# A two-block network on one core: first-stage transfers and matmul parts in a new order, key tiles in homes of their own

## The reference

```
mod = silu(c) @ w_ada + b_ada                    # c: 1 x 1024, w_ada: 1024 x 6144
shift1, scale1, gate1, shift2, scale2, gate2 = split(mod, 6)
h = x * (1 + scale1) + shift1                    # x: 256 x 1024
q, k, v, z, xbc, dt_raw, g = split(h @ w_in)     # q, k, v: 1024 columns each
...                                              # attention, scan, gating, experts, two more layers
```

## Time and profile before

| | |
|---|---|
| time, median of 3 runs | 1861.02 us (1858.63 to 1865.48) |
| the profiled execution's own time | 1863.23 us |
| its span | 1861.4 us |
| TensorE matmul busy | 1684.5 us (90%) |
| VectorE busy | 915.7 us (49%) |
| ScalarE busy | 568.4 us (31%) |
| mean granted TensorE clock | 0.965 of full |
| DMA | 563.19 MB, mean 303 GB/s |

### The profile page before, as it was taken

One profiled execution on the slowest core, in us unless ns is written; L12 is line 12 of the kernel. 1 busy time (PEld: TensorE's weight loads), 2 busy tenths in 40 slices (PEclk: granted clock), 3 DMA queues, 4 the chain that ended last, 5 costly groups with the idle time before them and its releaser, 6 DMA issues.

```text
span 1861.4 us, 30972 instructions
## 1 busy us (share of the span) xinstructions
PE 1684.5 (90%) x12554; PEld 1596.1 (86%) x12554; DVE 915.7 (49%) x2285; ACT 568.4 (31%) x1528; POOL 326.9 (18%) x301
## 2 busy tenths in 40 slices
PE   4999999999989888888898899777799999999998
PEld 4789878888888888877898899776699999989998
DVE  5642375651447666666877754469634210331200
ACT  0111223840135444434564321235513100132000
POOL 0100000000024444344423312126300000020000
PEclk9998999999999999989999999888899999999999
DMA  8963348354189999999999999999876888745783
GB/s 363 374 234 112 114 125 257 118 224 144 46 328 377 420 417 418 421 420 420 416 420 411 420 420 408 421 382 382 328 266 250 325 294 295 251 176 207 272 293 133
DMA packets 85437, 563.19 MB, mean 303 GB/s; under 512 B 8832, under 2 KB 17568, under 8 KB 17968
## 3 DMA queue, kind: packets, MB, share of 16 engines
q0 software_dynamic: 39776, 289.46, 38.0%
q1 hardware_dynamic: 38416, 251.85, 36.4%
q10 hardware_dynamic: 7104, 19.92, 3.4%
HBM read 556.96 MB, written 4.23 MB: 301 GB/s over the span
## 4 chain that ended last, share of the span: by engine, by line
PE 68%; DMA 15%; DVE 7%; ACT 6%; issue 3%; POOL 0%; SPq 0%; ACTq 0%; DVEq 0%; POOLq 0%
PE PS L965 30%; PE PS L655 19%; PE PS L944 8%; DMA AUX<-in_peer_uv_dram,SCR 4%; DMA V<-in_peer_uv_dram,SCR 4%; DMA CONV<-in_peer_uv_dram,SCR 4%; DMA ring<-in_stream_dram 3%; PE PS L726 1%; DVE PROJ L2203 1%; PE PS L701 1%; PE PS L677 1%; PE PS L859 1%; ACT L1503 1%; ACT PROJ L1518 1%; DVE SCR L2140 1%
## 5 line engine op out<-in xcount | busy, mean ns | idle before, releaser
L944 PE MATMUL PS<-PROJ,AUX 128*128 128x128 f32 x1712 | 223.5, 290 | 67.5 <-ACT PROJ L1518 67.3
L655 PE MATMUL PS<-H,ring 128*128 128x256 f32 x1216 | 274.9, 387 | 4.4 <-DMA ring<-in_stream_dram 4.4
L944 PEld LDWEIGHTS PS<-PROJ,AUX 128*128 128x128 f32 x1712 | 211.9, 203 | 75.4 <-ACT PROJ L1518 74.9
L655 PEld LDWEIGHTS PS<-H,ring 128*128 128x128 f32 x1216 | 235.2, 195 | 38.4 <-issue 5.9
L965 PE MATMUL PS<-H,ring 128*128 128x128 f32 x2272 | 261.7, 276 | 3.9 <-DMA ring<-in_stream_dram 2.2
L965 PEld LDWEIGHTS PS<-H,ring 128*128 128x128 f32 x2272 | 258.2, 193 | 5.1 <-issue 4.2
L1301 POOL DMA_INDIRECT AUX<-in_peer_uv_dram,SCR x124 | 138.9, 1120 | 485.1 <-PE PS L944 254.2
L944 PE MATMUL PS<-PROJ,CONV 128*128 128x128 f32 x1248 | 166.9, 294 | 41.7 <-ACT PROJ L1518 41.6
L944 PEld LDWEIGHTS PS<-PROJ,CONV 128*128 128x128 f32 x1248 | 159.7, 209 | 45.7 <-ACT PROJ L1518 45.5
L965 PE MATMUL PS<-PROJ,ring 128*128 128x128 f32 x1664 | 191.4, 275 | 2.7 <-DMA ring<-in_stream_dram 2.7
L965 PEld LDWEIGHTS PS<-PROJ,ring 128*128 128x128 f32 x1664 | 188.6, 192 | 3.8 <-DMA ring<-in_stream_dram 3.4
(11 more groups left out here) (351 smaller groups left out, 2033.5 us busy)
## 6 DMA issues: line engine op xcount, KB each, us to landing
ring<-in_stream_dram SPq DMA_DIRECT2D x181, 1024.0 KB
AUX<-in_stream_dram SPq DMA_DIRECT2D x51, 1024.0 KB, 4.8
AUX<-in_ada_dram POOLq DMA_DIRECT2D x16, 1024.0 KB, 9.4
PROJ<-in_ada_dram ACTq DMA_DIRECT2D x4, 1024.0 KB, 20.3
AUX<-in_ada_dram SPq DMA_DIRECT2D x4, 1024.0 KB, 20.0
AUX<-in_stream_dram ACTq DMA_DIRECT2D x4, 1024.0 KB, 8.3
bias_skewed<-AUX ACTq DMA_DIRECT2D x1, 3072.0 KB, 43.5
ring<-in_stream_dram ACTq DMA_DIRECT2D x2, 1024.0 KB
```

What stands on the lines that cost most here:

```text
L655: mm = pe.matmul(acc(n, c), w[:, k, c * P:(c + 1) * P], src[:, g * DC + k, :], start=(g == 0 and k == 0 and (c == 0 or groups == 1)), stop ...
L944: mm = pe.matmul(y_chunk(t, c), UV[b][:, D + c * P:D + (c + 1) * P], DIAG[turn % ND], start=(k == 0 and c % 4 == 0), stop=(k == SPT - 1), ...
```

## The change

Four edits, all in the first stage.

1. The four key tiles no longer pass through `ring`. They are loaded by ScalarE, behind its other first issues, into `KEY_HOMES`: three regions of `PROJ` (chunks 40 to 63) and all of `V`, which hold nothing yet at that time. TensorE waits for all four before the first key tile. The ring's counts are lowered by one to fit; SP's loop over the stream starts with the value tiles, and its waits on `tile_used` are as before.
2. The order of the first issues: SP gets `par`, shift 0, `X`, query 0, shift 1, query 2, shift 2, shift 3; ScalarE gets scale 0, `con`, scale 1, query 1, scale 2, query 3, scale 3, `rows`, `wdt` and the four key tiles. `con` is now counted with `X` and not with `par`; ScalarE's `silu(c)` waits for `par` alone but stands behind 13 issues; TensorE, GpSimd and `modulated(0)` wait for `X` and `con`.
3. On VectorE the first half of pair 2 moves ahead of `modulated(1)`.
4. The parts of the query projection are in another order around the column sums.

```diff
 def place(e):
-    before = FRONT // SLOTS if slot < SLOTS else 0
+    before = FRONT // SLOTS - 1 if slot < SLOTS else 0
...
+        KEY_HOMES = [flat(PROJ[:, 40:48, :]), flat(PROJ[:, 48:56, :]), flat(PROJ[:, 56:64, :]), flat(V[:, :, :])]
...
             shift_tile(0)
             sp.dma_start(X[:, :, :], io["xT"]).then_inc(S("x_landed"), 16)
+            query_tile(0)
             shift_tile(1)
-            query_tile(0)
+            query_tile(2)
             shift_tile(2)
-            query_tile(2)
             shift_tile(3)
-            with sp.Fori(1, TILE0["query"] // SLOTS) as i:
+            with sp.Fori(2, TILE0["query"] // SLOTS) as i:
...
             def tile_wait(name, i):
                 t = TILE0[name] + i
-                pe.wait_ge(S(f"tile_landed{t % SLOTS}"), 16 * (t // SLOTS + 1))
+                if name == "k":
+                    pe.wait_ge(S("homes_landed"), 64)
+                    return KEY_HOMES[i].rearrange("p (k n) -> p k n", k=DC)
+                pe.wait_ge(S(f"tile_landed{t % SLOTS}"), 16 * (t // SLOTS + (1 if name == "q" else 0)))
...
-            pe.wait_ge(S("params_landed"), 32)
+            pe.wait_ge(S("x_landed"), 32)
...
             early_sums(0)
             query_part((0, 1), (0, 1))
             early_sums(1)
+            query_part((2,), (0, 1))
             query_part((0, 1), (2, 3))
-            query_part((2,), (0, 1, 2, 3))
             early_sums(2)
-            query_part((0, 1), (4, 5))
+            query_part((2,), (2, 3))
+            query_part((3,), (0, 1))
             early_sums(3)
-            query_part((3,), (0, 1, 2, 3))
-            query_part((2, 3), (4, 5))
+            query_part((3,), (2, 3))
+            query_part((0, 1, 2, 3), (4, 5))
             query_part((0, 1, 2, 3), (6, 7))
...
-            act.dma_start(con[:, :], io["con"]).then_inc(S("params_landed"), 16)
             scale_tile(0)
-            act.dma_start(rows[:, :], io["rows"]).then_inc(S("rows_landed"), 16)
+            act.dma_start(con[:, :], io["con"]).then_inc(S("x_landed"), 16)
             scale_tile(1)
             query_tile(1)
             scale_tile(2)
+            query_tile(3)
             scale_tile(3)
-            query_tile(3)
+            act.dma_start(rows[:, :], io["rows"]).then_inc(S("rows_landed"), 16)
             act.dma_start(wdt[:, :, :], io["wdt"]).then_inc(S("wdt_landed"), 16)
-            act.wait_ge(S("params_landed"), 32)
+            for t in range(4):
+                act.dma_start(KEY_HOMES[t], io["stream"][TILE0["k"] + t]).then_inc(S("homes_landed"), 16)
+            act.wait_ge(S("params_landed"), 16)
...
             def ada_pair(p, ks=range(DC)):
...
             ada_pair(1)
+            ada_pair(2, range(0, 4))
             modulated(1)
-            ada_pair(2)
+            ada_pair(2, range(4, DC))
```

More of the change, by code:

```diff
@@ L852, in out_tile @@
                 if u == 0 and t == 0:
-                    pe.wait_ge(S("out_landed"), 64)
+                    pe.wait_ge(S("homes_landed"), 128)
                 ready = taken_from("ssd") if u == 0 and t == 0 else None
@@ L1252, in _ @@
                     pool.dma_start(flat(adaW[:, s]), io["ada"][4 * i + s]).then_inc(S(f"ada_late{s}"), 16)
-            pool.wait_ge(S("params_landed"), 32)
+            pool.wait_ge(S("x_landed"), 32)
             for h in range(HEADS):
@@ L1449, in _ @@
             for t in range(4):
-                act.dma_start(out_weights(t), io["stream"][TILE0["query"] + t]).then_inc(S("out_landed"), 16)
+                act.dma_start(out_weights(t), io["stream"][TILE0["query"] + t]).then_inc(S("homes_landed"), 16)
             for c in range(16):
@@ L1833, in ada, with ada_pair @@
                             ada_step(adaW[:, s], k, CONV[:, base + s, :], k and ada_done(i, s) - 2 * (DC - k))
-            def ada_pair(p):
+            def ada_pair(p, ks=range(DC)):
                 dve.wait_ge(S(f"ada_landed{p}"), 16)
                 dve.wait_ge(S(f"ada_early{p}"), 16)
-                for k in range(DC):
+                for k in ks:
                     for j, w in enumerate((adaW[:, p], adaE[:, p])):
@@ L1857, in modulated @@
                 if p == 0:
-                    dve.wait_ge(S("x_landed"), 16)
+                    dve.wait_ge(S("x_landed"), 32)
                 for c in (2 * p, 2 * p + 1):
```

## The result

The changed kernel took 1867.8 us (median of 7 runs, 1863.36 to 1874.08) against 1863.43 us for the kernel before, measured beside it (7 runs, 1858.63 to 1865.48). The ratio is 1.0033, 95% interval 1.0017 to 1.0048: 3 to 9 us slower, where 3 us faster was forecast. The median of the kernel before is, by these 7 runs, 2.4 us above the one that the prediction stood on.

What follows compares the result with a forecast made beforehand. Bound: the first-stage path through transfers, VectorE's sums and TensorE up to the keys' end. 3.8 us late against 7.4 saved gave -3.6, taken as -3: 1858 us from the median of 1861.02, range 1851.5 to 1864.

Steps and rivals of the forecast that it cites:

- The step that failed: ScalarE's start: four added issues of about 0.5 us each, silu done near 9.4 us in place of 7.34.
- The mechanism: Rival, chance 0.07: ScalarE's tenth to thirteenth issues wait for landings, silu ends at 24.4 us, keys +3.2 us, about 1864.
- The second term: TensorE's clock behind the thin stretch, 25 to 47 us: a loss between 0 and 3.0 us.
- the 16 matmuls ahead of `early_sums(3)` warm the clock first: Argument against the clock staying low on the 36 query matmuls behind the last sums, which would take 2 to 3 us.
- The missing gap: Ahead of the key projection: no 4.4 us wait for key tiles and no slow clock behind it, 7.4 us saved.
- the order of issues and of parts: Reordering in the first stage: last sums 2.0 us late, 36 matmuls behind them, query projection ends 3.8 us later.
- shift tile 2 was read off at 32.9 us: Transfer step in SP's queue: shift tile 2 lands at 32.9 us in place of 27.8, about 5 us later.
- for this move the prediction had under half a microsecond: Moving `rows` to the end of ScalarE's queue gives that queue 0.16 MiB, under half a microsecond.
- The rival in which this delay isn't felt: Rival, chance 0.08: shift tile 2 stays near 27.8 us, total change -6 to -7.6 us, about 1854.3.
- the slow rival: Rival, chance 0.07: waiting issues in ScalarE's queue hold silu and make the kernel 3.2 us slower, about 1864.
- the clock had a chance of its own: Rival, chance 0.14: the clock stays low behind the last sums, 2 to 3 us of the gain go, about 1860.5.

Runs made afterwards that it cites:

- x2: Kernel before with only the key tiles loaded to their homes, their issues ahead of silu; 1863.32 us, ratio 0.9994.
- x4: Kernel before, keys through the ring, plus four loads of 128 partitions by 8 bytes issued by ScalarE ahead of silu; 1868.72 us, one run.
- x5: Kernel before, keys through the ring, plus four loads of 16 partitions by 8 bytes issued by ScalarE ahead of silu; 1861.24 us, one run.
- r3_after: The changed kernel executed once more, nothing altered; 1871.98 us.
- x1: Changed kernel with silu moved ahead of ScalarE's four key-tile issues, nothing else; 1865.61 us, ratio 1.0001.
- x6: Changed kernel with the four key tiles issued by SP behind shift 3 in place of ScalarE; 1866.13 us, ratio 1.0014.
- x8: x3 with the changed kernel's order of first issues on SP and ScalarE, and `con` counted with `X`; 1863.04 us, ratio 0.9994.
- x3: Kernel before with only the key tiles loaded to their homes, silu ahead of their issues; 1858.43 us, ratio 0.9972.
- x7: x3 with VectorE's first half of pair 2 ahead of `modulated(1)` and the query parts in another order; 1859.53 us, ratio 0.9979.

## Why the prediction was wrong

**The step that failed.** "ScalarE issues 13 transfers in place of 9 before `silu`. The ninth cost 0.47 us; four more of about 0.5 put the end of `silu` from 7.34 to about 9.4 us." The four cost 13.8 us (5.77 to 19.57) and silu was done at 21.1. Nothing in the trace before showed a full queue, because no issuer there had more than nine transfers of 128 rows under way; x2 and x4 show that the eleventh to thirteenth wait for 3 to 4.3 us each (the tenth 0.4 to 1.2), and x4 and x5 that bytes and the number of transfers are not what fills the queue. The mechanism stood among the rivals with a chance of 0.07. Its rule, one waiting issue for each landing, is what the landings show; it put silu at 24.4 us, as it took the fourth landing for 22.4, where r3_after has 20.2 and an issue that was over at 19.3. Its price was +3.2 us, and the stage measured +3.0. But its own sum has nothing lost at 21 us, and here 3 us are lost at 21.1. That the sizes agree is partly luck. From silu at 21.1 its own steps put the last sums at 50.2 us, and they began at 50.1; what it left out is the slow clock behind them, 2.8 us on the 36 matmuls and 0.6 on the sums themselves.

**The second term.** The forecast took 0.6 us for the clock (-3 in place of -3.6), within bounds of 0 to 3.0. Against x1 it cost the changed kernel 3.3 us, and 1.7 in r3_after, more than the lateness of 1.6 and 1.3. That "the 16 matmuls ahead of `early_sums(3)` warm the clock first" was no protection. Between those matmuls and the sums TensorE waited 2.1 us for VectorE, and the clock fell behind that wait. In x1, x6 and x8, where that wait is shorter or absent, it fell earlier, where the path goes over VectorE, and the last matmuls ran at 2.4 GHz.

**The ladder.** One edit at a time, keys' end in the profiled executions:

| kernel | what is added to the one above | keys end us | step |
|---|---|---|---|
| before | | 95.7 | |
| x3 | key homes, silu ahead of their issues | 89.1 | -6.6 |
| x8 | edit 2, the changed order of first issues | 91.3 | +2.2 |
| x1 | half pair ahead of `modulated(1)`, query parts reordered | 93.7 | +2.4 |
| after | key issues ahead of silu | 98.7 (96.7 in r3) | +5.0 (+3.0) |

**The other steps.** The missing gap, 7.4 us, was right (6.6 measured in x3, keys at 27.63 us, none late). That the order of issues and of parts costs 3.8 us was right in direction: x8 and x1 show 4.6 together. One term was mis-sized: shift tile 2 was read off at 32.9 us and landed at 34.6 (x1, x8), shift tile 1 at 22.8 and landed at 24.6, and in x1 the query projection ended at 66.1 us and not 64.6. The prediction gave each queue half of the rate and counted MiB in one queue alone. In the profiles the two queues went in step instead: of the first eight, the n-th transfer of SP and the n-th of ScalarE landed within 1 us of each other wherever the profile has both, whatever their size (before, `X` with 1024 KB at 13.0 us and `rows` with 160 KB at 13.3). Moving `rows` back put scale 1, a whole tile, beside `X`, and `X` landed at 14.7 us in x8; for this move the prediction had under half a microsecond. An estimate from the two queues together: before, shift 2 was SP's sixth transfer, and SP's and ScalarE's first six are 9.84 MiB; in the new order it is the seventh, and the first seven of both are 12.68 MiB. The 2.84 MiB more are 7.1 us at 421 GB/s, and it landed 6.8 us later (34.6 against 27.8), where the prediction had 5.1. The rival in which this delay isn't felt is excluded by the same rows. The forecast's whole sum was -3.6 us; x1, which is the changed kernel without the held silu, has -2.0 us, and the late tiles are the difference.

**From the stage to the total.** 3.0 us of the stage and 1.7 us of clock behind the dt matmuls make 4.7 us, which the span shows (4.6), and lie in the interval of 3 to 9 us; with r3's 96.7 us it would be 2.7. The range ended at 1864 because the price of the slow rival was set on the median of 1861.02 with nothing added for the clock or for later stages, though the clock had a chance of its own.

The first scan product shows stage and stretch together. Each row is one profiled execution against 337.6 us of the kernel before; the last column is the 95% interval of the totals, turned into us.

| kernel | keys end | first scan product | total, interval |
|---|---|---|---|
| after | +3.0 | +4.6 | 3.2 to 8.9 |
| x1 | -2.0 | -0.4 | -1.7 to 2.2 |
| x2 | -1.3 | +0.3 | -3.5 to 1.3 |
| x3 | -6.6 | -5.0 | -7.6 to -2.8 |
| x6 | -2.0 | +1.0 | 0 to 5.2 |
| x7 | -7.4 | -7.4 | -6.3 to -1.5 |
| x8 | -4.4 | -2.8 | -3.9 to 1.7 |

In six of the seven the total agrees with what the profile has at the first scan product (r3_after alone would put the changed kernel at +2.6). x7 lost 1 us or more behind it, for which no cause was shown. The spread of the expert stage from one execution to the next, 829 to 838 us, is as large as any of this, so a single total says nothing here. x1 and x6, 2 us faster at the keys' end, are not faster in total.

## What to carry to other kernels

A transfer is cheap to issue only while its issuer's queue has room, here nine to ten transfers of 128 rows. Count the rows that stand in it, and put everything that other engines wait for ahead of the first issue that may wait. Here moving one activation ahead of four issues is worth 3 to 5 us at the keys' end. In total it takes the changed kernel from a loss to no measurable change (x1), and edit 1 alone from no measurable change (x2) to a gain of about 5 us (x3), which is the part of the change worth keeping. When all DMA engines are full, a tile moved ahead is paid for by the tile behind it (x8, 2.2 us), so order transfers by who is on the path.

## What the runs showed of the hardware

- Up to the ninth transfer of 128 rows an issue from ScalarE took 0.4 to 0.5 us (the fourth 0.7 to 1.0). In the changed kernel the tenth to thirteenth took 1.2, 4.0, 4.3 and 4.3 us. It was the same for 8-byte rows (x4, four in 11.53 us) and not for loads of 16 rows (x5, four in 2.54 us). SP's eleventh and twelfth took 3.8 and 4.25 us (x6).
- A waiting issue ended within 1 us of one landing of the same issuer's queue, in order (6.7, 10.7, 15.0 and 19.3 us against 6.5, 10.3, 15.2 and 20.2 in r3_after).
- With both queues moving (50.7% and 50.5% of the DMA engines), SP's and ScalarE's transfers landed in pairs, the n-th with the n-th, whatever their size: in the kernel before at 5.1 and 4.6 us (173 and 520 KB), 9.9 and 10.4, 13.0 and 13.3 (1024 and 160 KB), 17.8 and 18.3.
- Where TensorE's clock falls is repeatable to a degree: the stretch behind the first scores took 214.3 us in three executions of one kernel, and 216.0 and 215.9 in two of another that does the same work there. In the same two executions of the second kernel the slow clock around the last sums cost 3.3 and 1.7 us.
